# One change to a hybrid encoder kernel: Q of levels 1 to 4 of a block inverse as T turned by transposes

## The reference, cut to what matters

```python
def step(state, inp):
    r_t, w_t, k_t, v_t, kk_t, a_t = inp
    sa = jnp.einsum('bhvk,bhk->bhv', state, kk_t)
    state = (state * w_t[:, :, None, :]
             - sa[..., None] * (kk_t * a_t)[:, :, None, :]
             + v_t[..., None] * k_t[:, :, None, :])
    y = jnp.einsum('bhvk,bhk->bhv', state, r_t)
    return state, y
```

## Time and profile before

| | before |
|---|---|
| median of 3 runs | 4602.02 us |
| profiled execution, its own time | 4605.25 us |
| its span, first to last instruction | 4603.5 us |
| TensorE busy, matmuls | 4251.3 us, 92% |
| VectorE busy | 1597.5 us, 35% |
| ScalarE busy | 1286.1 us, 28% |
| GpSimd busy | 302.0 us, 7% |
| mean granted TensorE clock | 0.972 |
| mixer steps with their sections | from about 137 to 3070 us |

### The profile page before, as it was taken

How to read it: one execution, slowest core, us unless ns; L and a number is a source line. 1 busy time by engine, 2 the same in 40 slices (tenths; PEclk the granted TensorE clock), 3 DMA queues, 4 the chain that set the end, 5 groups by cost and what they waited for, 6 DMA issues and landing times.

```text
span 4603.5 us, 91439 instructions
## 1 busy us (share of the span) xinstructions
PE 4251.3 (92%) x36699; PEld 2261.7 (49%) x36699; DVE 1597.5 (35%) x3205; ACT 1286.1 (28%) x2931; POOL 302.0 (7%) x391
## 2 busy tenths in 40 slices
PE   7999999999999999999999999989959999999992
PEld 4455555555555555555555555555534444444441
DVE  3333433343334334433343344333341111111115
ACT  5123333333333333333333333334311111111113
POOL 0000100010000000000000000000000000000003
PEclk9999999999999999999999999999969999999996
DMA  9101000100100100100100100024349999999999
GB/s 327 44 6 50 10 11 28 32 9 21 36 13 9 48 8 13 46 11 9 50 9 11 32 27 9 9 73 133 128 170 410 411 411 411 411 411 411 411 411 379
DMA packets 251006, 628.35 MB, mean 136 GB/s; under 512 B 11410, under 2 KB 96628, under 8 KB 250612
## 3 DMA queue, kind: packets, MB, share of 16 engines
q1 hardware_dynamic: 231956, 555.46, 32.1%
q0 software_dynamic: 11520, 41.95, 2.3%
q10 hardware_dynamic: 7136, 25.23, 1.3%
HBM read 561.75 MB, written 60.84 MB: 135 GB/s over the span
## 4 chain that ended last, share of the span: by engine, by line
PE 86%; issue 5%; DVE 4%; ACT 2%; DMA 2%; SPq 1%; DVEq 0%; POOL 0%; POOLq 0%; ACTq 0%
PE bank L944 38%; PE bank L1288 10%; PE bank L1292 5%; PE bank L1318 5%; PE bank L1158 4%; PE duo L1069 4%; PE bank L1322 2%; PE duo L1058 2%; PE duo L1056 1%; PE duo L1269 1%; DMA adaw<-in_w_ada_dram 1%; ACT xs L1354 1%; PE bank L1001 1%; PE duo L881 1%; PE bank L985 1%
## 5 line engine op out<-in xcount | busy, mean ns | idle before, releaser
L944 PE MATMUL bank<-hT,w 128*128 (+1 forms) x4096 | 1791.2, 594 | 0.0
L944 PEld LDWEIGHTS bank<-hT,w 128*128 128x128 f32 x4096 | 777.5, 190 | 995.0 <-issue 995.0
L1288 PE MATMUL bank<-W,xT 128*128 128x512 f32 x1024 | 446.6, 594 | 2.2 <-DVE xT L2249 1.5
L1354 ACT ACT_TABLE_LOAD x254 | 325.9, 1283 | 25.3 <-DVE ub L1934 14.3
L1288 PEld LDWEIGHTS bank<-W,xT 128*128 128x128 f32 x1024 | 192.7, 191 | 233.4 <-issue 233.4
L2255 DVE TENSOR_TENSOR gsig<-bank,gsig 128x512 f32<-128x512 f32 x48 | 33.2, 691 | 673.7 <-ACT gsig L1354 673.7
L1292 PE MATMUL bank<-W,xT 128*64 128x512 f32 x1024 | 227.2, 598 | 18.6 <-issue 18.6
L1158 PE MATMUL bank<-wo,mT 128*128 128x512 f32 x512 | 232.3, 600 | 0.0
L1318 PE MATMUL bank<-W,aT 128*128 128x512 f32 x512 | 225.1, 592 | 0.0
L720 POOL TENSOR_TENSOR Tm<-Tm,idents 128x512 f32<-128x512 f32 x32 | 40.5, 1266 | 2809.7 <-DVE Tm L1967 2809.7
L1069 PE MATMUL duo<-Qm,Zm 64*64 64x64 f32 x5120 | 197.2, 227 | 21.7 <-issue 14.1
(11 more groups left out here) (370 smaller groups left out, 5508.2 us busy)
## 6 DMA issues: line engine op xcount, KB each, us to landing
W<-in_w_expert_in_dram SPq DMA_DIRECT2D x128, 2048.0 KB, 25.5
W<-in_w_expert_out_dram SPq DMA_DIRECT2D x64, 2048.0 KB, 25.4
w<-in_w_in_dram SPq DMA_DIRECT2D x64, 512.0 KB, 4.0
adaw<-in_w_ada_dram SPq DMA_DIRECT2D x12, 2048.0 KB, 12.8
y_s<-ysb ACTq DMA_DIRECT2D x48, 512.0 KB, 6.7
xt<-in_x_dram SPq DMA_DIRECT2D x16, 512.0 KB, 12.0
WAc<-rank_s SPq DMA_DIRECT2D x32, 256.0 KB, 3.3
GDc<-rank_s SPq DMA_DIRECT2D x32, 256.0 KB, 3.3
```

The costliest lines, as they stand in the source:

```text
L944: ins = mm(PJ[j % 2][:, :], w[:, j, k, :], hT[:, k, ds(group(i) * G, G)], start=k == 0, stop=k == KT - 1)
L1288: ins = mm(GU[half][:, :], xT[:, slot, kk_, :], ring_rows(parts[0])[:, k, cols], start=kk_ == 0, stop=kk_ == KT - 1)
L1354: return nc.scalar.activation(o, i, f, **kw)
```

## The change

Q of levels 1 to 4 is no longer computed by a product and two subtractions. It is the transpose of T, so four 128x128 transposes (QT, two 64-column blocks by two heads each) turn Tm, and the result is copied into Qm: bank 0 by VectorE, bank 1 by ScalarE. For that Tm is now stored with the two heads of a slot side by side (`T_of`). Q of level 5 stays a product. QT of level n stands in SCHED behind Z of level n + 1 and the hop after it, where TR stood; the TR items move on by half a level, to where Q stood. T of level n + 1 (and Q of level 5) waits for QT of level n.

```diff
-    return [("Z", lv, (0, 1)), hops[0], ("TR", lv - 1, (0, 1)), hops[1], ("T", lv, (0, 1)), hops[2],
-            ("Q", lv, (0, 1)), hops[3]]
+    return [("Z", lv, (0, 1)), hops[0], ("QT", lv - 1, (0, 1)), hops[1], ("T", lv, (0, 1)), hops[2],
+            ("TR", lv, (0, 1)), hops[3]]
...
-    plan += level(1, [n[5], None, n[6], n[7]])
+    plan += [("Z", 1, (0, 1)), n[5], ("TR", 0, (0, 1)), ("T", 1, (0, 1)), n[6], ("TR", 1, (0, 1)), n[7]]
     for lv in range(2, 5):
         plan += level(lv, n[4 * lv:4 * lv + 4])
-    plan += [("Z", 5, (0, 1)), n[20], ("TR", 4, (0, 1)), n[21], ("TR", 5, (0, 1)), n[22], ("Q", 5, (0, 1)), n[23]]
+    plan += [("Z", 5, (0, 1)), n[20], ("QT", 4, (0, 1)), n[21], ("TR", 5, (0, 1)), n[22], ("Q", 5, (0, 1)), n[23]]
...
+def on_act(u):
+    return u[0] == "TR" or (u[0] == "QT" and u[2] == 1)
...
+        def Q_of(p, b):
+            return Qm[p][:, :, :].rearrange("p (a k) t -> p k a t", a=2)[:, 2 * b:2 * b + 2]
+        def turned_in(u):
+            return bank(u)[:, 0:2 * P].rearrange("p (k a t) -> p k a t", k=2, a=2)
...
+            def turned_T(lv):
+                for k in range(4):
+                    bk = bank(("QT", lv, k // 2, 0))
+                    ins = tr(bk[:, k % 2 * P:k % 2 * P + P], Tm[:, 2 * k:2 * k + 2, :].rearrange("p h t -> p (h t)"),
+                             ident[:, :])
+                    if k % 2:
+                        ins.then_inc(S["gram_done"], 1)
...
-                            ins = mm(one, LTb[p][rows, e, HD:2 * HD], Tm[rows, e, :], start=True, stop=True)
+                            ins = mm(one, LTb[p][rows, e, HD:2 * HD], Tm[rows, 2 * k + h, :], start=True, stop=True)
...
+                    if what == "use" and name == "QT":
+                        u = ("QT", more[0], 1, 0)
+                        wait_gram(act, i, u)
+                        fn(Q_of(p, 1), turned_in(u), ACT.Copy).then_inc(S["tok_copied"], 1)
...
-                        ins = V.tensor_tensor(Tm[:, cs, :], Tm[:, cs, :], bk, ALU.subtract)
+                        ins = V.tensor_tensor(T_of(b), T_of(b), bk, ALU.subtract)
+                    elif kind == "QT":
+                        ins = V.tensor_copy(Q_of(p, b), turned_in(u))
```

More of the change, by code:

```diff
@@ L80, in pair_of @@
     return 1 if u[0] in ("LT", "Z", "T") or u[:2] == ("TR", 5) else 0
-ON_ACT = [u for u in PLAN if u[0] == "TR"]
-ON_DVE = [u for u in PLAN if u[0] != "TR"]
+def on_act(u):
+    return u[0] == "TR" or (u[0] == "QT" and u[2] == 1)
+ON_ACT = [u for u in PLAN if on_act(u)]
+ON_DVE = [u for u in PLAN if not on_act(u)]
 def build(nc, io, out):
@@ L1022, in operands_of @@
                     return [("LT", 0, b, 0)] if lv == 1 else [("T", lv - 1, b, 0)]
[L1023 to L1026, removed]
+                if kind in ("T", "Q"):
+                    return [("Z", lv, b, 0)] + ([("QT", lv - 1, b, 0)] if lv > 1 else [])
+                if kind == "QT":
+                    return [("T", lv, b, 0)]
                 return []
@@ L1097, in product @@
                     turned(kind, lv, p)
+                elif kind == "QT":
+                    turned_T(lv)
                 elif kind == "Q":
@@ L1959, in over, with T_of @@
                     return m.unsqueeze(1).to_broadcast([P, n, m.shape[1]])
+                def T_of(h):
+                    return Tm[:, :, :].rearrange("p (k h) t -> p h k t", h=2)[:, h]
                 def evacuate(kind, lv, b):
@@ L1966, in evacuate @@
                     if kind == "L":
-                        ins = V.tensor_tensor(Tm[:, cs, :], bk, over(m0s[:, :], 4), ALU.mult)
+                        ins = V.tensor_tensor(T_of(b), bk, over(m0s[:, :], 4), ALU.mult)
                     elif kind in ("LT", "GK"):
@@ L2007, in step @@
                                 done = n + 1
-                            evacuate(name, more[0], 1)
+                            if name != "QT":
+                                evacuate(name, more[0], 1)
                             if name == "LT":
```

## The result

The changed kernel takes 4554.5 us (median of 4 runs, 4551.8 to 4555.8) against 4602.9 us for the kernel before (four runs now): a ratio of 0.990, 95% interval 0.9887 to 0.9912. That is 48 us less, where 18 were forecast. The profiled execution took 4554.68 us.

The account below looks back on a forecast made before the run. TensorE, busy 92% of the span, was taken to bound the kernel, with short waits and stalls. Terms -19 + 1.5 - 8 + 8 = -17.5 us gave 4587.75 for the profiled execution, 4584 as median; range 4550 to 4616.

Parts of the forecast that it names:

- rival (c): Sections: 1.3 us of TensorE work, 0.4 of waits and a 0.5 stall go each; 4534, likelier 4557; chance 0.14.
- the clock: Sparser levels 1 to 4 bring 5 more falls of the granted clock at 1.5 us each, 8 us slower.
- the walk: Level-by-level timing of a section with recurrence: 0.6 us gained in each of 31 sections, 19 us.
- the first section: Section without a recurrence: nothing covers QT, T comes 0.4 us later in four levels, +1.5 us once.
- The transposes' price: Four QT transposes hold TensorE 0.62 us against Q's 0.85, so its work falls 0.9 us per step.
- levels 1 and 2: Sections, from x2 and from Z2: gain 0 in both; in the second, T waits 0.34 us for the copy.
- level 4: Section, from u5 to Z5: 3.27 us against 3.45 before, Q's 0.27 wait for a TR copy gone; gain 0.2.
- level 3: Section, from Z3 to x5: 3.69 us against 3.97 before, with QT held until TR 2 is copied; gain 0.3.
- Rival (a): Sections: waits for QT and its copies eat the whole gain; 4594 to 4604, given as 4600; chance 0.18.
- Fewer instructions: Sections: 13% fewer TensorE instructions cut 2.5 us of fetch stalls by 0.25 us each, 8 us, bounds 0 and 20.
- rival (b): Sections: sparser TensorE work brings up to 36 more clock falls of 1.5 us, 54 us; time 4630; chance 0.19.

Follow-up runs that it names:

- the offsets: Both kernels with 0, 64, 128 or 192 semaphore increments (also 32, 256) at the start of TensorE's program, shifting later code; gains 48, 41, 28, 104 us at the quarter offsets.
- N = 0: Both kernels without added increments at the start of TensorE's program: 4602.9 us before, 4554.5 us after.
- N = 128: Both kernels with 128 semaphore increments added at the start of TensorE's program, outside every loop: 4651.3 us before, 4622.9 us after.
- N = 192: Both kernels with 192 semaphore increments added at the start of TensorE's program, outside every loop: 4684.9 us before, 4580.9 us after.
- N = 64: Both kernels with 64 semaphore increments added at the start of TensorE's program, outside every loop: 4641.9 us before, 4601.4 us after.

## Why the prediction was right or wrong

The sign was right and the size was not: 18 us forecast, 48 measured, 55 over the offsets. The nearest case was the likelier two thirds of rival (c), 4557, which I gave too little; but its mechanism did not come (TensorE's work fell by less than its 1.3 us, and the waits grew), so the match of the number is luck. In the span 33 us more went than forecast. Of these, 16 lie in the stalls (-24 against -8), 17 in the clock (-9 against +8) and 12 outside of the sections, where I had nothing; the walk gave 8 less and the first section lost 4 more. The stalls are the step that failed by the change's own doing, the clock and the stretches outside by the place of the code. Step by step:

- **The transposes' price: right.** A QT of four is one group of 0.63 to 0.66 us, and the next work starts 0.55 to 0.60 us behind its start; I took 0.62. The copies take 425 ns on VectorE and 383 on ScalarE (0.38 to 0.42).
- **The walk: right in levels 1 and 2, half in level 4, wrong in level 3.** In the section from 1183.8 us Z 2 starts 1.27 us behind x2 (1.28 forecast), T of level 2 2.58 us behind Z (2.61), and Z 3 4.62 behind Z 2 (4.69). In level 4 Z 5 starts 3.35 us behind u5 (3.27), so 0.1 of the 0.2 us was won. These rows are level 3:

```profile
1199.52 0.63 PE L1057 MATMUL duo<-ident,Tm 128*128 128x128 f32 x4 [0.27 <-ACT tok L1378]
...
1200.71 0.33 PE L1080 MATMUL duo<-Zm,Qm 64*64 64x64 f32 x4 [0.19 <-ACT Qm L1378]
1201.29 0.62 PE L1080 MATMUL duo<-Zm,Qm 64*64 64x64 f32 x27 [0.25 <-issue]
```

 QT starts 1.07 us behind Z 3, held by TR's copy (0.95 forecast), T 2.26 (2.15), and x5 4.29, or 4.04 without the stall, where I had 3.69: before it was 3.97, so the 0.3 us of this level were not won. The term that was wrong there is QT's start behind the copy of TR 2, and what stands behind it. Over all levels TensorE's busy time fell by 0.51 us a section at N = 0 and 1.0 over the offsets (0.9 forecast), and the waits ate 0.2 to 0.3 of it. The walk gave 0.3 to 0.4 us a section at N = 0, -11 us against my -19. Over the offsets it is 0.7 (1.0 less 0.3) against my 0.6, but since up to 0.8 us of busy time come and go with the place alone, that agreement may be luck. Rival (a), the waits eat it all, is refuted: 0.2 us is the largest wait at T.
- **Fewer instructions: the term that failed.** I took 13% of 2.5 us of stalls, 0.25 us a section, -8 us with a bound of 20. The stalls fell by 0.8 us a section (24 us in the 30) at N = 0, and over the offsets by 1.0 us a section (1.3 in those without a fall), 30 to 40 us. Two faults lie in it. The stalls are not a share of the instruction count: with 13% fewer instructions 31 to 38% of them went over the offsets (3.2 to 2.2 us, and 3.4 to 2.1), but 16% at N = 128 and over 60% at N = 192. And I read one arrangement of the code as if it were the kernel's nature; of the five different places, N = 0 has the least stalls, 2.4 us; with the code elsewhere I would have read 3.5 to 3.8. That the reading of the stalls as code arriving was right is now shown by the period of 256 and by the packets that land before them. The "mostly hidden" of the Trainium skill (Runtime: NRT & Kernel Launch, "Instruction fetch mechanics") doesn't hold in these sections, where 1.4 to 3.8 us of 29 to 32 were stalls; its block of 256 instructions in 16 KiB does.
- **The clock: wrong in sign at N = 0, and no effect of the change in the 30 sections that could be told.** I had 5 falls more, +8 us. The sections lost 9 us less to it, but only 1.5 us less in the mean over the offsets, with +18 at N = 64 and -19 at N = 192. So no effect of the change on the falls in these sections can be told, and rival (b) with its 36 falls more is refuted; my 5 falls more are within what the place does. By the rule that stood beside it in the Trainium skill (TensorE: Matmul & The Clock Gate, Part 4) more would have been lost at each offset; it was more at 64 and 128 and less at 0, 32, 192 and 256. The first section lost more than I had (+5.4 against +1.5), with 20 us at 0.50; over the offsets it is 26.0 against 23.1 us, +2.9. There the change may have an effect: its granted clock is 0.60 to 0.67 at 0, 128, 192 and 256 and 1.00 at 32 and 64, where the kernel before never has less than 0.89.
- **Between the sections** I had nothing, and 8 us went (61.36 to 61.07 us each). The kernel before has 61.07 to 61.22 at the offsets 32 to 192 and 61.36 at 256, so it is the place of its code too.

What stays open: why the change takes away a third of the stalls with 13% of the instructions. Of the blocks 0.9 a section went (7072/32/256, and 6.1 to 5.2 packets), of the stalls 0.75 (3.1 to 2.4), and those left are shorter. Which blocks bring a stall probably depends on what TensorE runs while they are under way. That it is the count and not the new order is not shown: the order alone, with every instruction kept, had 1.7 us of stalls too, at its one place. I didn't try a kernel with Q left out altogether, nor a filler that costs TensorE nothing inside the section.

## What to carry to other kernels

Where an engine runs hundreds of short instructions in 30 us, time the two versions at three or four offsets of the code before believing a gain or a loss of 1%: a few dozen do-nothing instructions ahead of the loops, behind a first transfer, cost next to nothing, and where the code lay moved one and the same kernel by up to 2 us a section. Read the idle time that no releaser explains as a budget of its own, look whether instruction packets land before it, and don't price it by the share of instructions: here that share was 13% and the stalls fell by 16% to over 60%, as the code lay. And when a change has two halves (another operation, another order), price the wait of each half alone: here each lost 1% at its one place of the code and both together win 1%.

## What the runs showed of the hardware

- TensorE's stalls have a period of 256 instructions in the offset of the code, 0.3 to 1.9 us each, mostly at the same instruction in every round of a loop; the profile names some of them after a releaser that had been done before.
- 958 of 959 such stalls end 1.2 to 1.8 us after a 16384-byte packet has landed on the instruction queue; about half of these packets bring a stall (3.1 of 6.1 a section in the kernel before).
- A semaphore increment in TensorE's queue costs 0.10 us in a row of 86 between two projections and 0.14 us in a row of 56 in the section; ten single ones fewer in each of 32 sections gave 4 and 16 us, 0.01 to 0.05 each.
- With the same work in each section, the place of the code goes with how often the granted clock falls to 0.50: between 5 and 45 us were lost to it in the 30 sections of the changed kernel.
